# Feeding the products of a recurrent scan's projections to TensorE in twos

## The reference

```python
def rwkv_prepare(h, mu, w_in, ...):            # h: 512 tokens, context and input
    xx = centred_shift(h)
    lerp = lambda j: h + xx * mu[j]
    r = heads(lerp(0) @ w_in[0])               # j = 0
    k = heads(lerp(1) @ w_in[1])               # j = 1
    v = heads(lerp(2) @ w_in[2])               # j = 2
    gate = lerp(3) @ w_in[3]                   # j = 3
...
# wkv_scan: for every head a 64x64 state is carried over the tokens, forwards and backwards
# rwkv_readout: group norm of the scan's output, plus a bonus term, times silu(gate), @ w_out
```

## Time and profile before

| | us |
|---|---|
| runs of the kernel | 2570.5, 2577.51, 2576.24; median 2576.24 |
| profiled execution | 2568.52, of which the span is 2566.8 |
| TensorE busy in the span | 2276.0 (89%) |
| mean granted TensorE clock | 0.937 |
| the scan's matmuls in the span | from about 1424 to 2197 |

### The profile page before, as it was taken

How to read it: one execution, slowest core, us unless ns; L and a number is a source line. 1 busy time by engine, 2 the same in 40 slices (tenths; PEclk the granted TensorE clock), 3 DMA queues, 4 the chain that set the end, 5 groups by cost and what they waited for, 6 DMA issues and landing times. The chain is left out here.

```text
span 2566.8 us, 40218 instructions
## 1 busy us (share of the span) xinstructions
PE 2276.0 (89%) x16920; PEld 1682.1 (66%) x16920; DVE 974.0 (38%) x2194; ACT 522.6 (20%) x926; POOL 319.0 (12%) x558
## 2 busy tenths in 40 slices
PE   2999966789999999999998688999998899879998
PEld 1888855578788886688873345565566667446546
DVE  3124436430343057277316244424424531120253
ACT  1011012320100010200013334333333422011142
POOL 0000000000000030000003544333432011000000
PEclk9999987799999999999999789998999889889989
DMA  7455520414686421187504665545544241313100
GB/s 298 184 225 218 197 100 0 81 23 161 273 303 232 177 104 50 66 332 297 207 1 163 215 171 161 148 124 139 137 122 110 49 112 44 150 51 117 47 1 17
DMA packets 126267, 359.75 MB, mean 140 GB/s; under 512 B 78600, under 2 KB 87048, under 8 KB 108304
## 3 DMA queue, kind: packets, MB, share of 16 engines
q1 hardware_dynamic: 93776, 213.05, 24.2%
q0 software_dynamic: 31744, 143.16, 16.5%
q10 hardware_dynamic: 576, 1.05, 0.1%
HBM read 340.36 MB, written 16.85 MB: 139 GB/s over the span
## 5 line engine op out<-in xcount | busy, mean ns | idle before, releaser
L271 PE MATMUL bank<-h,ring 128*128 128x256 f32 x2944 | 638.2, 380 | 4.8 <-DVEq L975 3.3
L271 PEld LDWEIGHTS bank<-h,ring 128*128 128x128 f32 x2944 | 560.3, 190 | 84.7 <-DVEq L975 4.9
L1755 PE MATMUL bank<-rw_feed 128*128 128x512 f32 x464 | 255.4, 658 | 22.3 <-DMA rw_feed<-in_rkvg 22.2
L185 PE MATMUL bank<-con 128*128 128x512 f32 x290 | 142.7, 644 | 91.9 <-PEq L257 57.6
L1571 POOL DMA_DIRECT2D rw_feed<-rwkv_mixes x232 | 124.5, 537 | 501.2 <-PE bank L1755 492.0
L185 PEld LDWEIGHTS bank<-con 128*128 128x128 f32 x290 | 58.0, 204 | 160.9 <-issue 160.3
L885 PE MATMUL bank<-ffn_hidden,ring 128*128 128x256 f32 x704 | 152.4, 379 | 3.4 <-PEq L911 3.4
L2056 DVE TENSOR_TENSOR rw_u<-bank,rw_lam 128x128 f32<-128x128 f32 x120 | 35.0, 291 | 301.8 <-PE bank L1702 298.3
L885 PEld LDWEIGHTS bank<-ffn_hidden,ring 128*128 128x128 f32 x704 | 133.6, 190 | 22.2 <-issue 4.1
L1755 PEld LDWEIGHTS bank<-rw_feed 128*128 128x128 f32 x464 | 79.3, 200 | 88.4 <-issue 45.7
L1572 POOL DMA_DIRECT2D rw_feed<-in_rkvg x232 | 124.2, 535 | 10.1 <-issue 10.1
(11 more groups left out here) (394 smaller groups left out, 3304.2 us busy)
## 6 DMA issues: line engine op xcount, KB each, us to landing
ring<-in_stream SPq DMA_DIRECT2D x81, 2048.0 KB, 8.1
rw_feed<-rwkv_mixes POOLq DMA_DIRECT2D x232, 256.0 KB, 3.0
next_w<-in_mod_stream POOLq DMA_DIRECT2D x24, 2048.0 KB, 10.4
ctx<-in_mod_rest POOLq DMA_DIRECT2D x16, 1024.0 KB, 7.2
rw_feed<-in_rkvg POOLq DMA_DIRECT2D x232, 64.0 KB, 3.2
rwkv_mixes<-mixed SPq DMA_DIRECT2D x8, 1024.0 KB, 3.9
y<-bias_table SPq DMA_DIRECT2D x48, 128.0 KB, 4.8
rw_at<-rw_at_kept SPq DMA_DIRECT2D x16, 256.0 KB, 5.7
```

Of the source, the lines that this page charges most:

```text
L185: pe.matmul(k.psum[bank][:], const(k, "ident"), k.con[:, 0:512], start=True, stop=True)
L271: mm = pe.matmul(out, ring_tile(k, n, kt, i * P), rhs[kt], start=start and kt == kts[0], stop=stop and kt == kts[-1])
L1755: pe.matmul(k.psum[PROJ], feed[:, g % FEED, 512:], feed[:, g % FEED, 0:512], start=(kt == 0), stop=(kt == KT - 1)).then_inc(eaten, 1)
```

## The change

`scan_project` now gives four `proj` entries per projection in place of eight, kt = 0, 2, 4, 6, and the TensorE branch issues two products, kt and kt + 1, for each. So a slot with four projections holds sixteen entries. All products, their DMAs and their arithmetic stay. As the list is shorter, its entries get other places: the first pair stands at 0.1 of the stretch where single products stood at 0.05 and 0.16, the last at 0.7, and the `rows` item at 0.9 in place of 0.944.

```diff
 def scan_project(n, j):
-    return [("proj", n, j, kt) for kt in range(KT)] + [("rows", n, j)]
+    return [("proj", n, j, kt) for kt in range(0, KT, 2)] + [("rows", n, j)]
...
                 elif kind == "proj":
-                    projected(n, *item[2:])
+                    for kt in range(item[3], item[3] + 2):
+                        projected(n, item[2], kt)
```

## The result

| | before | after |
|---|---|---|
| median of the runs | 2576.39 us (2570.5 to 2577.51, 4 runs) | 2593.52 us (2586.7 to 2594.5, 4 runs) |
| profiled execution | 2568.52, span 2566.8 | 2586.7, span 2584.9 |
| PE busy, granted clock | 2276.0 us, 0.937 | 2280.0 us, 0.932 |

The account below looks back on a forecast made before the run. TensorE was taken as nearly always busy, alternating with waits for DVE or ACT. Terms -2.2 - 0.8 - 0.9 + 4.8 = +0.9, plus +10.7 for the clock, gave +11.6 us: median 2587.8 us, 8-in-10 range 2570 to 2603.

Parts of the forecast that it names:

- (b): Slots 1 to 3: low clock lasts through chain 5 and gr, 2.0 us a slot, +6.0 us; bounds 0 and 3.5.
- Part 1: Fewer tile-shape changes on TensorE: -2.2 us in slots 0 to 3, -0.8 before chain starts, -0.9 in slots 6 and 7.
- Chain 13: Behind kk 2: arrives 0.85 us later, so DVE's scaling and whole stretch start about 0.37 us late.
- ACT costs nothing: Last btok evacuation waits some 4 us longer behind the rows item, but its copy is through before bonus needs the bank.
- R3: Rival: all 51 tile-shape changes pay, also under waits, and no product loses cover: -8.6 us, 2567.6; chance 0.04.
- Part 2: Slots 4 and 5: three single products each leave the cover of waits, +2.4 us a slot, +4.8 us.
- Part 3: Granted clock of TensorE: +7.2 in slots 4 and 5, +6.0 in slots 1 to 3, -2.5 at slot 5 to 6; +10.7 us.
- (a): Slots 4 and 5: clock falls at gr, 3.6 us a slot, +7.2; bounds 0, and 7 a slot if already at second gram.
- R2: Rival: clock no longer falls at gr in slots 1 to 3, denser work ahead of read 4: -9.9, 2566.3; chance 0.06.
- (c): Slot 5 to 6: the 23.8 us low-clock stretch ends 5 us sooner, half gained, -2.5 us; bounds 0 and -6.
- R1: Rival: the clock keeps its pattern, only stops saved and cover lost count: +0.9 us, 2577.1; chance 0.34.
- R4: Rival: POOL's feed runs out at ends of slots 0 to 3, 1 us for each of 16 pairs: +17, 2593; chance 0.03.

Follow-up runs that it names:

- experiment 7: Change plus btok issued three times in slots 1 to 5: 1.0032; with atok seven times too: 0.9942, beside the nearly alike filled kernel without the change, 0.9902.
- experiment 5: Pairs except in the gates of slots 4 to 7, with one product ahead of chain 13 and three behind in slots 0 to 3: 2573.14 us, 0.9992 of before.
- experiment 4: Kernel before, with one gate product (kt 2) moved from ahead of btok to behind gr in slots 4 and 5 only: 2587.57 us, 1.0046.
- Experiments 3: The change, with the last btok ahead of gr issued three times in slots 4 and 5: 2593.64 us, 1.0094 of before.
- kernel 1 of experiment 1: The change, but the gates of slots 4 to 7 in single products at their old places: 2575.21 us, 1.0009 of before.
- experiment 1's second half: Kernel before, with pairs only in the gates of slots 4 to 7: 2596.62 us, 1.0093.

## Why the prediction was right, and where it was not

The forecast of 2587.8 us and the range (2570 to 2603) hold the result, 2593.5, which lies 5.7 above the point. The sign, the slots and the two causes (lost cover and the clock) were right for slots 4 and 5: forecast there 4.8 + 7.2 = 12.0 us, measured 11.8. All else was forecast at -0.4 us and came to +6.3 (fill and slot 0 +3.95, slots 1 to 3 -2.4, the end of the scan +0.3, behind the scan +4.4). That the total still comes near is in part luck: the +6.0 of (b) did not come in this execution, and time that was not forecast stands in its place. Term by term:

**Part 1, -3.9 us forecast, about 0 found.** The stops do save what was forecast: in slot 2 of the two kernels of experiment 7, 0.34 us until kk 2 in spite of 0.44 and 0.26 us of waits for ACT (bonus, kk 0) and 0.20 more at the second gram; so 0.34 + 0.90 = 1.24 us, against 0.92. Chain 13 takes back 0.52 (forecast 0.37), as experiment 5 confirms. What failed is the sentence that ACT costs nothing: "the copy is through" when bonus needs its bank holds only while gr runs at the low clock. Ahead of slot 0 it is larger: a kk 0 waits 1.30 us for ACT, before the change 0.25, and a gr further on 0.88, before the change not at all:

```profile
1543.06 1.05 PE L1595 MATMUL bank<-rw_half,rw_ee 128*128 128x2 f32 x8 [1.30 <-ACT rw_ee L1866]
```

Net +0.2 and +0.1 us in slots 2 and 3 in place of -0.55 each. (The prediction takes 0.16 us a change, but its 0.92 for six changes and the 0.17 of R3 are not quite that; nothing hangs on it.)

**Part 2, +4.8 forecast, about 4.5 found** (2.1 + 2.4, experiment 7, where up to 1.7 us a slot were set down to the clock; and 0.86 for one product, experiment 4, against 0.85). The waits of 2.50 and 1.86 us answer to the forecast of some 2.4 and 1.9. This is the firmest part.

**Part 3, +10.7 forecast; about 14 found between the two profiled executions.** By the page's figures the clock was low for 2 x (1 - 0.937) x 2566.8 = 323 us before and 2 x (1 - 0.932) x 2584.9 = 352 after. If work at the lower level (1.2 GHz) takes twice as long (gr took 4.27 us in place of 2.29), 28 us more are up to 14 us of time, and some 4 of the 18.1 are left for parts 1 and 2. That is an upper bound, since low clock under a wait for DVE costs nothing.
- (a) Slots 4 and 5, +7.2 forecast. The size holds (11.8 us in those rows, less some 4.5 of cover), the place only in part: the clock was low at gr for 3.4 us in each slot, and most of the rest stands elsewhere. Experiments 3 and 4 show why "the clock falls at gr" was too narrow: with the wait filled it stayed up at gr and fell later; with the wait at 1.86 us it stayed up at gr and fell later in slot 4, and fell at gr in slot 5. The bound that the prediction named, a fall at the second gram, came in slot 5 of after.
- (b) Slots 1 to 3, +6.0 forecast, none found in after. In slots 2 and 3 the stretch around gr is 13.7 us as forecast ("some 14"), but that at the first gram is 3.4 in place of 6.8. In slot 1 the clock did not fall at gr at all: what R2 had for all three slots came in one (that denser work ahead of read 4 is the reason, as R2 has it, is not shown). These slots came out 2.4 us shorter. In kernel 1 of experiment 1, whose code is the same here, they came out 2.3 us longer, with slots 2 and 3 longer by 3.1 and 3.2 us: there (b) is right in sign and place for two slots, and slot 1, 4 us shorter, takes most of it back.
- (c) Slot 5 to 6, -2.5 forecast. The stretch was 17.1 us (2105.3 to 2122.4) in place of 23.9, but up to the end of the scan the low clock is the same in sum: nothing.
- Not forecast: 4.4 us behind the scan. All other kernels but one show 49.7 to 51.5 us of low clock there, as after does, whether they hold the change or not; before, with 39.8, is one of two exceptions. So this is no effect of the change. How the executions without a profile stood there is not known, so these 4.4 us can't be taken off the 17.1 between the medians.

Rival R1 (+0.9, the clock keeps its pattern) is refuted by the result, 11 to 23 us slower by the interval with 28 us more of low clock, and again by experiment 1's second half. R3 is refuted by slots 2 and 3 in experiment 7, which gained nothing at the full clock. R4 is refuted by the waits for DMA, 56.4 us.

What stays open: what exactly decides where the clock falls. No run tells whether the longer waits or the pairs in unbroken work bring the low stretches of slots 4 and 5; experiment 4 has one of each, a longer wait and a pair behind gr. With both kinds of waits filled, 10 to 12.5 us of difference remain while parts 1 and 2 explain some 5. The wait at the second gram of those slots (1.31 to 2.50 us) was not filled in any run. The one profiled execution of each of the two kernels of experiment 7 also cannot tell a shift up to the start of slot 2 (4.1 us between them, with some 10 us more of low clock) from chance.

## What to carry to other kernels

Work that stands ahead of a wait for another engine was free here, and a regrouping of equal pieces moved some of it out: ask of every single piece which wait it fills. Pairing gave nothing measurable here even where no piece left its wait. On a TensorE that alternates between work and waits of 1 to 6 us, price the clock beside the waits: repeats of wide transposes under two kinds of waits gave 23.7 us here (0.99), more than any order of the real work that was tried. Expect a low stretch to move when one wait is filled; judge by the clock of the whole span and the medians of several runs, not by the one stretch.

## What the runs showed of the hardware

- The clock stayed at 1.00 past the same wait of 1.86 us in slot 1 of after and in slot 4 of experiment 4, and was 0.50 behind it in slots 1 to 3 of before and in slot 5 of experiment 4: a wait of that length ahead of gr is not enough by itself to bring it down at gr.
- Identical code lay up to 6.7 us apart between profiled executions (experiment 4; and slots 1 to 3 with pairs took 282.7 or 287.4 us), and runs of the kernel before from 2564 to 2582 us; one variant spread over 34 us.
- A lone fp32 product between small tiles costs 0.2 us more than its 0.85; of 1.24 us a slot so saved nothing reached the end of the slot.
